# MoBA's softmax probabilities: transposes and their PSUM copy moved from TensorE and ScalarE to VectorE

## The reference

```python
s_own = jnp.einsum('hqd,hkd->hqk', qc, k_own) * scale
s_own = jnp.where((kpos[None, :] <= qpos[:, None])[None], s_own, -jnp.inf)
p = jax.nn.softmax(jnp.concatenate([s_sel, s_own], axis=-1), axis=-1)   # s_sel: nothing but -inf here
o = jnp.einsum('hqnk,hqnkd->hqd', p_sel, v_sel) + jnp.einsum('hqk,hkd->hqd', p_own, v_own)
```

## Time and profile before

| | |
|---|---|
| median of 3 runs | 2409.6 us (2409.42 to 2409.64) |
| profiled execution | 2409.38 us |
| its span, first to last instruction | 2407.6 us |
| TensorE busy | 2400.7 us (100%) |
| VectorE busy | 1803.6 us (75%) |
| ScalarE busy | 1237.7 us (51%) |
| GpSimd busy | 321.1 us (13%) |
| MoBA's heads, first scores to last product with the values | 152 to 329 us of the span |

### The profile page before, as it was taken

The page is one execution under the profiler, slowest core; times in us unless marked ns, Lnnn a source line. Parts: engine busy times, 40 slices in busy tenths (PEclk is TensorE's granted clock), DMA queues, the critical chain, the costliest instruction groups (busy, mean ns, idle before and its releaser), DMA issues.

```text
span 2407.6 us, 34025 instructions
## 1 busy us (share of the span) xinstructions
PE 2400.7 (100%) x10845; PEld 1983.8 (82%) x10845; DVE 1803.6 (75%) x2488; ACT 1237.7 (51%) x1597; POOL 321.1 (13%) x281
## 2 busy tenths in 40 slices
PE   9999999999999999999999999999999999999999
PEld 7888888888888888888888888888887888888887
DVE  5467679897888988988888897567767645587584
ACT  6445454555455444444444455455557555655443
POOL 0021242244210000000000000011101000521050
PEclk9999999999999999999999999999999999999999
DMA  7555555576655655565566656955554555555655
GB/s 272 192 187 180 174 177 175 185 250 221 227 191 184 201 192 195 193 194 193 185 192 199 193 190 215 254 183 179 177 184 163 178 163 176 178 170 166 227 192 166
DMA packets 134826, 464.24 MB, mean 193 GB/s; under 512 B 14544, under 2 KB 21328, under 8 KB 134112
## 3 DMA queue, kind: packets, MB, share of 16 engines
q1 hardware_dynamic: 122464, 443.08, 56.5%
q10 hardware_dynamic: 12256, 20.15, 2.7%
q0 software_dynamic: 32, 0.03, 0.0%
HBM read 455.87 MB, written 7.34 MB: 192 GB/s over the span
## 4 chain that ended last, share of the span: by engine, by line
PE 98%; DVE 1%; issue 0%; DMA 0%; ACT 0%; ACTq 0%; SPq 0%; DVEq 0%
PE PS L678 21%; PE PS L680 21%; PE PS L679 21%; PE PS L923 7%; PE PS L924 7%; PE PS L925 7%; PE PS L944 3%; PE PS L943 3%; PE PS L945 3%; PE PS L792 1%; PE PS L763 1%; PE PS L719 0%; PE PS L770 0%; DMA X<-x_in 0%; PE PS L1096 0%
## 5 line engine op out<-in xcount | busy, mean ns | idle before, releaser
L1157 ACT ACTIVATE WH<-RAW 128x1024 fp32r<-128x1024 f32 x841 | 888.9, 1059 | 1078.7 <-PE PS L680 685.8
L1711 DVE TENSOR_TENSOR WL<-RAW,WH 128x1024 fp32r<-128x1024 f32 x811 | 1020.9, 1266 | 537.3 <-ACT WH L1157 526.9
L678 PE MATMUL PS<-WH,HT 128*128 128x512 f32 (+1 forms) x1816 | 717.2, 395 | 0.2 <-issue 0.2
L680 PE MATMUL PS<-WH,HT 128*128 128x512 f32 (+1 forms) x1816 | 706.3, 389 | 0.0
L679 PE MATMUL PS<-WL,HT 128*128 128x512 f32 (+1 forms) x1816 | 705.4, 388 | 0.0
L678 PEld LDWEIGHTS PS<-WH,HT 128*128 128x128 f32 x1816 | 341.0, 188 | 72.6 <-issue 4.7
L680 PEld LDWEIGHTS PS<-WH,HT 128*128 128x128 f32 x1816 | 340.8, 188 | 71.1
L679 PEld LDWEIGHTS PS<-WL,HT 128*128 128x128 f32 x1816 | 341.2, 188 | 67.2
L923 PE MATMUL PS<-WH,HT 128*128 128x512 f32 x704 | 274.0, 389 | 0.0
L925 PE MATMUL PS<-WH,HT 128*128 128x512 f32 x704 | 273.9, 389 | 0.0
L924 PE MATMUL PS<-WL,HT 128*128 128x512 f32 x704 | 273.9, 389 | 0.0
(11 more groups left out here) (317 smaller groups left out, 2304.4 us busy)
## 6 DMA issues: line engine op xcount, KB each, us to landing
RAW<-w_stream SPq DMA_DIRECT2D x841, 512.0 KB, 3.5
bias_scratch<-BE ACTq DMA_DIRECT2D x12, 256.0 KB, 4.0
MEMR<-mem_in ACTq DMA_DIRECT2D x1, 2048.0 KB, 11.3
X<-x_in ACTq DMA_DIRECT2D x4, 512.0 KB, 4.6
x_scratch<-X ACTq DMA_DIRECT2D x4, 512.0 KB, 4.9
X<-x_scratch ACTq DMA_DIRECT2D x1, 2048.0 KB, 9.8
out<-X ACTq DMA_DIRECT2D x8, 256.0 KB, 3.2
X<-x_in SPq DMA_DIRECT2D x3, 512.0 KB, 9.2
```

Source lines behind the costliest of these rows:

```text
L678: pe.matmul(o, hi, WH[:, slot, kk, 0:cols], start=k == 0, stop=False)
L680: ins = pe.matmul(o, lo, WH[:, slot, kk, 0:cols], start=False, stop=k == nq * GK - 1)
L1157: act.activation(WH[:, g.slot(j)], RAW[:, g.slot(j)], ACT.Copy).then_inc(hi_split, 1)
L1711: dve.tensor_tensor(WL[:, s], RAW[:, s], WH[:, s].bitcast(F32), ALU.subtract).then_inc(lo_split, 1)
```

## The change

In MoBA alone, the probabilities are no longer transposed by TensorE in step 6 and copied by ScalarE. VectorE transposes them from PR to PT, SBUF to SBUF, with 16 instructions of three 32 x 32 blocks each ("32x96"): the eight that read partitions 0 to 63 of PR in step 4, behind the scaling, and the other eight in step 5, behind its split. The last of them signals pt_ready, for which L781 waits on TensorE in step 7. The other branches keep their way (`head_probs`).

```diff
+        TURNED_PROBS = [MOBA, ]
...
                 ins.then_inc(scores, 1)
+                if any(br is b for b in TURNED_PROBS):
+                    pe.sem_inc(pt_done, 1)
...
-            def moba_probs(H, M):
-                pe.wait_ge(probs_scaled, M.count(1))
-                head_probs(MOBA, H)
...
-                    elif p - 8 * r == 6:
-                        moba_probs(H, At(r, i, 2))
...
-                    st = head_steps(MOBA, At(MOBA0 + r, i, 2), At(r, i, 2), i * 2 + r, None, (None, 3, 6, 7))
+                    st = head_steps(MOBA, At(MOBA0 + r, i, 2), At(r, i, 2), i * 2 + r, None, (None, 3, None, 7))
...
-            def moba_scale(H):
+            def moba_scale(H, M):
                 dve.wait_ge(probs, H.count(1))
                 link(dve.reciprocal(RI[:], RS[:]))
                 dve.tensor_scalar(PR[:, 0:P], PR[:, 0:P], RI[:, 0:1], None, ALU.mult)
                 dve.tensor_scalar(PR[:, P:CAUS], PR[:, P:CAUS], RI[:, 1:2], None, ALU.mult).then_inc(probs_scaled, 1)
+                dve.wait_ge(probs_scaled, M.count(1))
                 dve.sem_inc(o_rows, 1)
+
+            def probs_turn(H, n, quarters):
+
+                dve.wait_ge(probs, H.count(1))
+                for a in quarters:
+                    for b in range(4):
+                        src = PR[32 * a:32 * a + 32, 0:n].rearrange("p (n s) -> p n s", s=P)[:, :, 32 * b:32 * b + 32]
+                        dst = PT[32 * b:32 * b + 32, 0:n].rearrange("p (n s) -> p n s", s=P)[:, :, 32 * a:32 * a + 32]
+                        ins = dve.transpose(dst, src)
+                if 3 in quarters:
+                    ins.then_inc(pt_ready, 1)
...
                     elif s == 4:
-                        moba_scale(H)
+                        moba_scale(H, At(r, i, 2))
+                        probs_turn(H, CAUS, (0, 1))
+                    elif s == 5:
+                        probs_turn(H, CAUS, (2, 3))
```

## The result

| | before | after |
|---|---|---|
| median | 2409.6 us (5 runs, 2409.42 to 2409.68) | 2435.6 us (5 runs, 2431.71 to 2435.76) |
| profiled execution / span | 2409.38 / 2407.6 us | 2434.02 / 2432.2 us |
| mean granted clock of TensorE | 1.000 | 0.996 |

The changed kernel is 26.0 us slower, a ratio of 1.0104 (95% interval 1.0093 to 1.0115). The forecast was slower by 11.7 us with a range to 2429. The direction was right and the size was not. The first sign of what else happened is the spread: the runs of before lie within 0.3 us, those of the changed kernel within 4.

What follows compares the result with a forecast made beforehand. TensorE, busy 100% of the span, bounds the kernel. Eight heads at net 1.4 us (11.2) plus 0.5 for the last head add 11.7 to 2409.38, so 2421.1; median 0.2 higher, 2421.3 us (+0.49%), range 2415 to 2429.

Steps and rivals of the forecast that it cites:

- TensorE's saving: Three 128x128 transposes a head leave TensorE: 0.33 us a head, 2.6 us in eight heads.
- The price of the transposes: VectorE's 32x96 transposes in steps 4 and 5: 0.27 us each, pitch 0.28, eight in 2.23 us.
- put PT in time: Rival: turned probabilities ready before TensorE needs them at L781, leaving only its saving, 2407.0 us; chance 5%.
- The wait ahead of L781: TensorE waits for VectorE's PT ahead of the product with the values: 1.66 us in head 0.
- the dearer bound: 1.26 us instead of 1.15 between split and transpose, used in the rival "VectorE doesn't catch up": 2428 us, 8%.
- the restarts: Behind each wait TensorE's second matmul comes 0.31 us later instead of 0.23: 0.08 us a head.
- The clock: Rival: each new wait throws TensorE to 1.2 GHz, 1.6 us a head, 13 us in all: 2434 us; chance 5%.
- The pause that ends at 1416.43: TensorE pause in the trace before, followed by a pitch of 0.31 and not 0.43 us; cited against the clock rival.
- What is late next: VectorE's later splits and turns queue behind the added work, but it catches up; delays don't add up between heads.
- the 1.2 us that I counted as spare: VectorE's margin at the next head's scores, having caught up after the added transposes: about 1.2 us.
- The last head: Head 7 dearer, its scaling later and splits slowed while GpSimd rotates for retention: 0.5 us taken, 0.39 sure.

Runs made afterwards that it cites:

- experiment 6: Kernel before without TensorE's 24 transposes and nothing in their place (ScalarE copies zeros to PT, MoBA's output left out): 2406.63 us.
- experiments 4, 5 and 12: Changed kernel with eight, four and two matmuls a head, results unread, ahead of L781's wait: 2424.54, 2424.73 and 2424.59 us.
- longer wait: Changed kernel with eight more 32x96 transposes a head, into a spare tile, ahead of the last eight: 2458.2 us.
- experiment 1: Changed kernel with all 16 transposes in step 4, none behind the split of step 5: 2416.25 us.
- experiment 7: Kernel before with 16 more VectorE transposes a head in steps 4 and 5, into an unread spare tile: 2414.09 us.

## Why the prediction was wrong

*TensorE's saving.* Right: 0.37 us a head, 2.9 us (forecast 0.33 and 2.6), by experiment 6.

*The price of the transposes.* Right: a pitch of 0.28 us and 270 ns for a shape that the trace before did not have, from the line through two other sizes. The Trainium skill's one element per cycle and lane ("Vector Engine (DVE) Microarchitecture Reference", section 3.8), taken alone and without a fixed part for each instruction, would have put PT in time. The trace doesn't agree with that: 270 ns an instruction and 2.25 us for eight.

*The wait ahead of L781.* Right in place and kind, in all eight heads; its size was off by 0.38 us a head. The forecast had 1.66 us between TensorE's earliest and its real start of L781, with the start's latency; measured are 2.04 (2.265 less a pitch of 0.23), and 0.4 us of the 16.8 is head 7's surplus. Three small gaps make up most of it: the first transpose starts 0.16 us behind the scaling's end and not 0.05; the first transpose behind a split starts 1.26 us after it and not 1.15, which the prediction had as the dearer bound; and L781 starts 0.14 us behind PT's end (163.95 + 2.26 to 166.35) and not 0.05. The 0.38 us cost 3 us in eight heads, and the restarts 1.0 us instead of 0.6. Had this been all, the time would have been 2424.6 us, that of experiments 4, 5 and 12, inside the range.

*The clock: the step that failed.* The prediction gave the fall of the clock 5% and put nothing for it into the sum. It was the difference between 2424.6 and 2435.6 us. That rival's price, 1.6 us a fall, was right. That its time, 2434 us, came so near was partly luck: its wait was 3 us too short and it had eight falls, where the profile has six and the median execution by its time seven. What was wrong is the evidence set against it. The pause that ends at 1416.43 is 1.12 us from matmul to matmul; the forecast one is 1.66 + 0.23 = 1.89 us, and the real one 2.27. The short one says nothing of the long ones. Nor was it enough to look at the first pitch behind the restart: it is 0.31 us there, and in head 0 of the changed kernel it is 0.31 us as well (167.00 to 167.31), and the clock falls all the same a quarter of a microsecond later. The experiments put the pauses beside each other. Distance from the last matmul, filling included, to L781, heads in which the clock fell in the profile, and median (of all executions, so it can hold a fall more or less than the profile):

| version | distance, us | falls | median, us |
|---|---|---|---|
| before | 0.23 | 0 of 8 | 2409.6 |
| all in step 4 | 1.01, head 7 2.30 | 0 of 8 | 2416.3 |
| eight matmuls as filling | 0.45 to 0.84 | 0 of 8 | 2424.5 |
| four | 1.34 to 1.75 | 0 of 8 | 2424.7 |
| two | 1.80 to 2.19 | 0 of 8 | 2424.6 |
| changed kernel | 2.27 to 2.63 | 6 of 8 | 2435.6 |
| longer wait | 4.39 to 4.76 | 8 of 8 | 2458.2 |

By how little it was missed is to be seen in the table: with 0.4 us less of standing still the clock stays up, but for one fall in one of four executions. The forecast distance of 1.89 us lies in that row. So the two errors probably belong together, the gaps of 0.1 us having carried the pause to where the clock mostly falls; a kernel with just the forecast pause wasn't run.

The Trainium skill, "TensorE: Matmul & The Clock Gate", Part 1, says that idleness brings the 1.2 GHz state back. The trace agrees: the clock is at 1.00 ahead of each pause of 2.27 us and more in the changed kernel, and at 0.50 behind six of the eight. The length of the pause alone doesn't decide it: heads 1, 3, 5 and 6 all have 2.28 us, and the clock falls in 3 and 5 and stays up in 1 and 6, as it does in head 7 of experiment 1 with 2.30 us. No experiment here varies when a pause comes, so what else decides stays open.

*What is late next.* Right for the changed kernel (VectorE waits for ScalarE again at 175.45), but only thanks to the wait. Experiment 7 shows that without it VectorE's round is 23.78 us, longer than TensorE's 23.49, so the 1.2 us that I counted as spare came from the wait.

*The last head.* The forecast surplus of 0.5 us is there as 0.35 (2.63 against 2.28 us).

## What to carry to other kernels

Moving work from the engine that bounds a kernel to one that is "75% busy" is decided by where its result is due: walk the dependent chain in the second engine's queue, and count every 0.1 us between unlike instructions, since a forecast of the pause is also a forecast of the clock. Price a new pause on TensorE as the pause plus a possible stretch at half the clock, and take a pause that was harmless as evidence only for pauses as short. Before giving a change up for it, look for the idle time that the second engine spends on something else at the head of its queue: the same 128 transposes, placed in front of a split that had to wait anyway, took the loss of 26 us away, and with retention's first transposes spread as well there was a small gain, 2.6 us.

## What the runs showed of the hardware that was not expected

- The clock need not fall at once: in head 0 of the changed kernel the matmuls run at full speed for 1.2 us behind the restart at 166.35 before the rate halves, while in the version with a pause of 4.4 us it is down before the pause ends.
- Matmuls whose result nobody reads were a gain inside a wait: two in each head, 0.45 us of work, made the changed kernel 11 us faster.
- The fall depends on the run: the five executions of the changed kernel lie between 2431.71 and 2435.76 us at mean clocks of 0.995 and 0.996, and one of four with two filling matmuls had one.
- VectorE's transposes weren't slowed beside GpSimd here: the first eight of head 7 take 2.25 us as in head 0, with GpSimd busy for 1.89 us of them (not at all in head 0), while a scaling in head 7, also beside GpSimd, takes 0.57 us instead of 0.29.
